# Attention with the keys on the partitions, and two output tiles of a projection begun slice by slice

## The reference, cut to what matters

```python
# first block: projection of the heads' output, y_b is 1040 x 1024
merged = (jax.nn.sigmoid(p[..., o5:o6]) * (y_a @ w_ssm_proj[l])
          + jax.nn.sigmoid(p[..., o6:]) * (y_b @ w_hgrn_proj[l]))

# second block: 8 heads, 1024 queries, 1280 keys (256 of the context), 96 dims, 64 values
def one(qi):
    s = jnp.einsum('bqhd,bkhd->bhqk', qi, k, preferred_element_type=jnp.float32) * scale
    p = jax.nn.softmax(s, axis=-1).astype(v.dtype)
    return jnp.einsum('bqhk,bkhd->bqhd', p, v)
...
yd = attn * jax.nn.silu(d_gate)
```

## Time and profile before

| | us |
|---|---|
| median of three runs (lowest, highest) | 3601.41 (3597.78, 3604.99) |
| the profiled execution | 3603.62 |
| its span in the profile | 3601.8 |
| TensorE busy | 3289.2 (91%) |
| VectorE busy | 2008.2 (56%) |
| ScalarE busy | 943.8 (26%) |
| GpSimd busy | 227.4 (6%) |
| TensorE idle in heads_out ahead of L795 | 35.6 |
| exponentials of the attention, first to last start | 3031.7 to 3391.1 |

### The profile page before, as it was taken

The page is one execution under the profiler, slowest core; times in us unless marked ns, Lnnn a source line. Parts: engine busy times, 40 slices in busy tenths (PEclk is TensorE's granted clock), DMA queues, the critical chain, the costliest instruction groups (busy, mean ns, idle before and its releaser), DMA issues. The chain is left out here.

```text
span 3601.8 us, 47693 instructions
## 1 busy us (share of the span) xinstructions
PE 3289.2 (91%) x20158; PEld 3042.2 (84%) x20158; DVE 2008.2 (56%) x2814; ACT 943.8 (26%) x1178; POOL 227.4 (6%) x224
## 2 busy tenths in 40 slices
PE   3999999999688779999999999899988996988887
PEld 3999999999677679999999999899988983555465
DVE  5565655566568444566446446645445535666446
ACT  3222222222323331121111111221133314444323
POOL 0000000000005200000000000000012000222200
PEclk9999999999798789999999999999989997999898
DMA  3222222222343344321321321411121321000031
GB/s 100 91 78 75 90 85 86 90 89 74 137 102 50 95 170 135 129 77 53 106 81 46 108 79 38 153 37 43 50 74 37 128 87 74 1 1 1 22 133 69
DMA packets 102463, 285.76 MB, mean 79 GB/s; under 512 B 13157, under 2 KB 32101, under 8 KB 101993
## 3 DMA queue, kind: packets, MB, share of 16 engines
q1 hardware_dynamic: 102248, 282.70, 24.6%
HBM read 218.68 MB, written 63.98 MB: 78 GB/s over the span
## 5 line engine op out<-in xcount | busy, mean ns | idle before, releaser
L491 PE MATMUL mixer_in_dense<-mix_z_high,mixer_in_whigh 128*128 128x348 f32 x1344 | 445.8, 332 | 11.3 <-POOL mixer_in_out L328 11.3
L491 PE MATMUL mixer_in_dense<-mix_z_high,mixer_in_wlow 128*128 128x348 f32 x1344 | 439.1, 327 | 0.0
L491 PE MATMUL mixer_in_dense<-mix_z_low,mixer_in_whigh 128*128 128x348 f32 x1344 | 438.2, 326 | 0.0
L1372 PE MATMUL flow_dense<-rst_norms_operand_b_high,flow_whigh 128*128 128x342 f32 x1248 | 399.2, 320 | 0.4 <-DVE flow_wlow L1464 0.4
L1372 PE MATMUL flow_dense<-irst_norms_operand_b_low,flow_whigh 128*128 128x342 f32 x1248 | 398.3, 319 | 0.0
L1372 PE MATMUL flow_dense<-rst_norms_operand_b_high,flow_wlow 128*128 128x342 f32 x1248 | 397.4, 318 | 0.0
L1930 PE MATMUL joint_dense<-rst_norms_operand_b_high,joint_whigh 128*128 128x342 f32 (+2 forms) x1056 | 344.7, 326 | 17.0 <-DVEq L2047 10.1
L1930 PE MATMUL joint_dense<-rst_norms_operand_b_high,joint_wlow 128*128 128x342 f32 (+2 forms) x1056 | 341.7, 324 | 0.0
L1930 PE MATMUL joint_dense<-irst_norms_operand_b_low,joint_whigh 128*128 128x342 f32 (+2 forms) x1056 | 340.6, 323 | 0.0
L1372 PE MATMUL flow_dense<-first_operand_a_high,flow_whigh 128*128 128x342 f32 (+1 forms) x912 | 291.4, 320 | 26.9 <-DVEq L1485 26.9
L1372 PE MATMUL flow_dense<-first_operand_a_low,flow_whigh 128*128 128x342 f32 (+1 forms) x912 | 291.8, 320 | 0.0
(11 more groups left out here) (544 smaller groups left out, 6201.3 us busy)
## 6 DMA issues: line engine op xcount, KB each, us to landing
mixer_in_wstage<-w_in SPq DMA_DIRECT2D x56, 512.0 KB, 4.6
mixer_in_mod_w<-w_mod SPq DMA_DIRECT2D x64, 384.0 KB, 3.6
first_norms_weights<-w_up SPq DMA_DIRECT2D x44, 512.0 KB, 3.5
flow_side<-h SPq DMA_DIRECT2D x24, 512.0 KB, 4.3
h<-flow_out SPq DMA_DIRECT2D x24, 512.0 KB, 3.2
first_norms_weights<-ab_w_in SPq DMA_DIRECT2D x20, 512.0 KB, 3.6
p<-mixer_in_out SPq DMA_DIRECT2D x16, 528.0 KB, 2.9
first_norms_weights<-w_down SPq DMA_DIRECT2D x16, 512.0 KB, 3.5
```

The lines of the kernel that those rows point to most:

```text
L491: mm = pe.matmul(pd[s % 2][:, 0:W], a[n % 2][:, P * m:P * (m + 1)], z[x][:, m, W * b:W * (b + 1)], start=m == 0 and i == 0, stop=m == DT - ...
L1372: mm = pe.matmul(o, w[n % NW][:, P * k:P * (k + 1)], x[h][:, k, where], start=k == 0 and e == 0, stop=k == kt - 1 and e == 2)
```

## The change

**heads_out.** `RING` is 6. TensorE computes slices 0 to 5 (tiles 0 and 1) together: for each piece k of `yb` 18 matmuls instead of 3, then slices 6 to 23 as before. The weights of tile 1 are loaded behind the first `yb` piece, and their high and low parts made ahead of piece 1. The small pieces of VectorE move in the table: one power behind each of the pieces 4, 5 and 6 and four behind the last, turns from 0 to 1, rotation and reverse from 1 to 2, coefficients from 2 to 3, the first table from 3 to 4, and later ones by about one slice.

**attend.** The work is in 16 units U of 512 queries of one head. `peak` computes high x high scores of 128 queries into three banks, of which VectorE takes only the maximum (`largest`); `rows` turns four such columns of maxima into a row of 512 by a product with the negated identity, and ScalarE copies it to one more row (number 96) of `query_high`, beside a row of ones in `key_high`. `chunk` k then computes the scores with 128 keys on the partitions and 512 queries on the free axis, the maximum already subtracted by the extra row; ScalarE makes exp straight into the operand of the value products, ten of 128x512 a unit. No transposes, no copies and no scaling by GpSimd are left. The sum over keys is made by four adds (`add_keys`) on GpSimd and a product with ones (`key_sums`) that spreads it over 64 partitions; VectorE's `finish` takes its reciprocal, multiplies it by the gate, adds the two halves of the value sums and multiplies.

The heads_out part, of the table `at` one line (turns 0 to 1, rotation and reverse 1 to 2, coefficients 2 to 3, table 3 to 4):

```diff
-    W, NP, NQ, RING = NM // 3, NPAIR, 8, 4
+    W, NP, NQ, RING = NM // 3, NPAIR, 8, 6
...
-                       (0, "turns", 0), (1, "rotation", 0), (1, "reverse", 0), (2, "coefficients", 0), (2, "negate", 0),
+                       (1, "turns", 0), (2, "rotation", 0), (2, "reverse", 0), (3, "coefficients", 0), (4, "table", 0),
...
                 for m in range(4):
                     load_yb(m)
+                    if m == 0:
+                        load(1)
                 for m in range(4, HH):
                     sp.wait_ge(x_low, m - 3)
                     load_yb(m)
-                load(1)
...
                 high(0)
                 for m in range(HH):
+                    if m == 1:
+                        high(1)
                     act.wait_ge(yb_landed[m % 4], 16 * (m // 4 + 1))
...
-                        if n + 1 < DT:
+                        if n and n + 1 < DT:
                             high(n + 1)
...
-                for s in range(NS):
+                def products(s, k):
                     n, b = divmod(s, 3)
-                    if b == 0:
-                        pe.wait_ge(low_ready, n + 1)
-                    if s >= RING:
-                        pe.wait_ge(moved, s - RING + 1)
+                    for e, (w, v) in enumerate(((wh, 0), (wl, 0), (wh, 1))):
+                        mm = pe.matmul(pd[s % RING][:, 0:W], w[n % 2][:, P * k:P * (k + 1)],
+                                       x[v][:, k, FIRST + W * b:FIRST + W * (b + 1)],
+                                       start=k == 0 and e == 0, stop=k == DT - 1 and e == 2)
+                    return mm
+
+                for k in range(DT):
+                    pe.wait_ge(x_low, k + 1)
+                    for s in range(6):
+                        if k == 0 and s % 3 == 0:
+                            pe.wait_ge(low_ready, s // 3 + 1)
+                        mm = products(s, k)
+                        if k == DT - 1:
+                            mm.then_inc(full, 1)
+                for s in range(6, NS):
+                    if s % 3 == 0:
+                        pe.wait_ge(low_ready, s // 3 + 1)
+                    pe.wait_ge(moved, s - RING + 1)
                     for k in range(DT):
+                        mm = products(s, k)
                     mm.then_inc(full, 1)
...
                 low(0)
                 for m in range(HH):
+                    if m == 1:
+                        low(1)
                     dve.wait_ge(x_high, m + 1)
...
-                    if b == 1 and n + 1 < DT:
+                    if n and b == 1 and n + 1 < DT:
                         low(n + 1)
```

The attention, its new functions and schedule:

```diff
+    def unit(U):
+        own = [[("e", U, k)] for k in range(NKT)]
+        first_, second_, third_ = made_at(U)
+        if U == 0:
+            for k in range(NKT):
+                own[k].append(("v", k))
+        if U + 1 < UNITS:
+            for q, k in enumerate((1, 3, 5, 7)):
+                own[k].append(("peak", U + 1, q))
+            own[6].append(("rows", U + 1, 0))
+        if U:
+            for p, k in enumerate((2, 3, 5, 7)):
+                own[k].append(("sums", U - 1, p))
+        own[2] += first_
+        own[4] += second_
+        own[8] += third_
+        if U + 1 < UNITS:
+            own[9].append(("rows", U + 1, 1))
+        if U:
+            own[9] += [("keys", U - 1), ("sums", U - 1, 4)]
+        return [n for k in own for n in k]
...
+        def add_keys(ch, tt, U):
+            p = PT[U % 2]
+            ch.do(tt(acc[:, :, :], p[:, 0:5, :], p[:, 5:10, :], ALU.add))
+            ch.do(tt(acc[:, 0:2, :], acc[:, 0:2, :], acc[:, 2:4, :], ALU.add))
+            ch.do(tt(acc[:, 0, :], acc[:, 0, :], acc[:, 1, :], ALU.add))
+            ch.do(tt(acc[:, 0, :], acc[:, 0, :], acc[:, 4, :], ALU.add))
...
+                def peak(U, q):
+
+                    h, b = divmod(U, 2)
+                    i = 4 * U + q
+                    if i:
+                        pe.wait_ge(maxed, i)
+                    q0 = HALF * b + P * q
+                    for k0, w in ((0, 512), (512, 512), (1024, 256)):
+                        mm = pe.matmul(pS[:, k0:k0 + w], qh[h % 2][0:KD, q0:q0 + P], kh[h % 2][0:KD, k0:k0 + w],
+                                       start=True, stop=True, skip_group_check=True)
+                    mm.then_inc(peaked, 1)
...
+                def rows(U, r):
+                    if U and r == 0:
+                        pe.wait_ge(rows_in, U)
+                    for q in (2 * r, 2 * r + 1):
+                        i = 4 * U + q
+                        pe.wait_ge(maxed, i + 1)
+                        mm = pe.matmul(pR[:, P * q:P * q + P], mx[:, i:i + 1], minus[:, :], start=True, stop=True,
...
+                def chunk(n):
+                    _, U, k = n
+                    h, b = divmod(U, 2)
+                    j, at, keys = h % 2, half_of(U), slice(P * k, P * k + P)
+                    if k == 0:
+                        pe.wait_ge(lows, HL.at(h, f"rope{b}"))
+                            pe.wait_ge(ones_in, 2)
+                        pe.wait_ge(rows_in, U + 1)
                     o = wait_free(pe, n)
+                    pe.matmul(o, kh[j][0:KD + 1, keys], qh[j][0:KD + 1, at], start=True, stop=False)
+                    pe.matmul(o, kl[j][0:KD, keys], qh[j][0:KD, at], start=False, stop=False)
+                    pe.matmul(o, kh[j][0:KD, keys], ql[j][0:KD, at], start=False, stop=True).then_inc(full, 1)
...
+                def value_sums(U, p):
+                    h = U // 2
+                    if p == 0:
+                        if U == 0:
+                            pe.wait_ge(v_made, 1)
+                        else:
+                            pe.wait_ge(y_added, U)
+                        pe.wait_ge(exped, NKT * (U + 1))
+                    for g in range(2):
+                        k = 2 * p + g
+                        mm = pe.matmul(pY[VD * g:VD * (g + 1), :], V[:, k, VD * h:VD * (h + 1)], PT[U % 2][:, k, :],
+                                       start=p == 0, stop=p == 4, skip_group_check=True)
+                    if p == 4:
+                        mm.then_inc(y_full, 1)
...
+                def key_sums(U):
+                    pe.wait_ge(added, U + 1)
+                    if U:
+                        pe.wait_ge(inverted, U)
+                    pe.matmul(pK, c["ones"][:, 0:VD], acc[:, 0, :], start=True, stop=True).then_inc(keys_full, 1)
...
+                def row(U):
+                    act.wait_ge(rows_full, U + 1)
+                    act.activation(qh[U // 2 % 2][KD:KD + 1, half_of(U)], pR, ACT.Copy).then_inc(rows_in, 1)
...
+                def largest(U, q):
+                    i = 4 * U + q
+                    dve.wait_ge(peaked, i + 1)
+                    dve.tensor_reduce(mx[:, i:i + 1], pS[:, 0:T2], AX.X, ALU.max).then_inc(maxed, 1)
+
+                def finish(U):
+                    h, at, own = U // 2, half_of(U), rows_of(U)
+                    dve.wait_ge(keys_full, U + 1)
+                    ch.do(dve.reciprocal(ri[own, :], pK))
+                    dve.sem_inc(inverted, 1)
+                    if U == 0:
+                        dve.wait_ge(gates_in, 64)
+                    ch.inc(tt(ri[own, :], ri[own, :], dg[own, h // 2, at], ALU.mult))
+                    dve.wait_ge(y_moved, U + 1)
+                    if h >= 2:
+                        dve.wait_ge(y_low, 2 * (h // 2 - 1) + U % 2 + 1)
+                    ch.do(tt(yp[own, at], pY[own, :], ytmp[own, :], ALU.add))
+                    dve.sem_inc(y_added, 1)
+                    ch.do(tt(yp[own, at], yp[own, at], ri[own, :], ALU.mult))
+                    dve.sem_inc(y_ready, 1)
...
+                ch = Chain(pool, pstep)
+                for U in range(UNITS - 1):
+                    pool.wait_ge(exped, NKT * (U + 1))
+                    if U:
+                        pool.wait_ge(keys_full, U)
+                    add_keys(ch, pool.tensor_tensor, U)
+                    pool.sem_inc(added, 1)
```

365 lines of the change are left out of this document (148 added, 217 removed).

## The result

The changed kernel takes 3658.18 us (median of 4 runs, 3656.11 to 3663.77) against 3599.6 us for the kernel before on the same chip: a ratio of 1.017 (95% interval 1.0156 to 1.0183), or 58.6 us more. Forecast were 3654, 53 above the median then known. The profiled execution has a span of 3654.7 us, 52.9 more than the one before.

A forecast was written before the change was run, and what follows sets the result against it. TensorE was taken to bound both changed places, its idle time being what could be won. Terms -12 (heads_out), +10 (finish) and +53 (hold) sum to +51; with 1 to 3 more at the end units, 3654 us, range 3590 to 3690.

The forecast's parts named there:

- The hold: Attention: GpSimd's adds lock the shared SBUF port against finish's product with the gate; TensorE waits 3.6 us a unit, +53.
- The reciprocal at 3.3 us: Attention, finish: VectorE's reciprocal of 64x512 takes 3.3 us, from 6.2 ns an element in the old rows.
- +10 without the hold: Attention: finish's chain alone exposes 1.2 us a unit, making units 23.2 us and the tail 2 to 3 longer.
- rival 1: No collision: GpSimd's adds meet finish too late or share the port without holding it; 3600 us, chance 0.13.
- The unit: Attention: 20.7 us of TensorE work at clock 0.94, plus 3.6 and 1.3 of waits, 26.9 or 27 a unit.
- The beginning: Attention: its beginning was taken to be about equal in length to before.
- heads_out: heads_out: slices 0 to 5 together keep TensorE busy; one wait of about 15 us for wlow, -12.
- rival 2: Attention: finish's chain is covered, a unit takes about 21.2 us; 3567 to 3580 us, chance 0.14.
- rival 3: Attention: GpSimd keeps the port through all four adds, VectorE never between; about 3690 to 3710 us, chance 0.10.
- A reading of the rows: Attention before: TensorE's 33.5 us idle ahead of transposes was put down to copies out of their banks.

The follow-up runs named there:

- the late adds: Changed kernel with GpSimd's adds of a unit waiting for the end of the previous unit's finish instead of its key sum: 3602.07 us, ratio 1.002.
- the heads_out part alone: Changed heads_out with attention as in the kernel before: 3578.27 us, ratio 0.995; run once more, 3574.98 us, ratio 0.9943.
- `finish` spread: Changed kernel with finish cut into pieces by urgency and its products of two SBUF inputs on GpSimd: 3567.48 us, ratio 0.991; once more 3564.43 us.
- the late adds and the copy: Changed kernel with GpSimd's adds waiting for the previous finish and a copy in place of the reciprocal: 3561.18 us, ratio 0.9895.
- the copy: Changed kernel with a copy in place of finish's reciprocal, leaving out the division by the sum: 3648.51 us, ratio 1.0151.
- `y_added` first: Changed kernel with finish reordered: sum of the two value halves first, then reciprocal, gate product, last product: 3657.2 us, ratio 1.0158.

## Why the prediction was right

- **The hold.** Right in mechanism and place, and shown: with the adds moved, or with one operand in another memory, L2733 falls to 0.69 and 51 to 57 us go, for a forecast of 53. Right in size at the wait, 3.5 us 14 times against 3.6, in part by two misses that cancel: `y_added` comes 6.6 us after the reciprocal's start, sooner than the 7.3 to 7.5 behind the key sum, and TensorE stands at its wait 3.3 us after that start instead of 3.8 behind the key sum.
- **The reciprocal at 3.3 us.** Right, 3.35. The Trainium skill (VectorE: DVE Perf Modes, "First, the fixed hardware budget") gives a repeat count of 8 and no duration. Read as eight passes over 512 elements, which was my reading and an estimate, it made 4.3 us; the trace does not bear that out: 3.35 us for 512 elements is 6.5 ns each.
- **+10 without the hold.** Mis-sized: with the late adds, and with the gate product reading PSUM, attention costs 24 and 26 us over the heads_out part alone. That their times, 3602.07 and 3601.04, stand at rival 1's 3600 is luck, since the kernel before took 3594.7 and 3594.5 beside them, 7 us less than the 3601.4 that the forecast started from, and heads_out gained more than 12. Written out, the +10 had only 5.6 for the units and 2 to 3 for the tail, 8 in all. What it lacked is in the late adds' trace: middle units of 24.9 us instead of 23.2 (TensorE idle 2.9 us in each instead of 1.2, at clock 0.94), and a first unit of 29.0 instead of 22.8, while the way to the first exponential is 2 to 3 shorter.
- **The unit.** Forecast 27, measured 28.6 in the middle. The mis-sized term is the clock on TensorE's own work. Its idle time is near the forecast: 4.6 us a unit, 3.5 of them for `y_added`, where 3.6 and 1.3 had been added. I took 20.7 us of work at a clock of 0.94, but the granted clock was 0.86, and 20.7/0.86 is 24.1 instead of 22.0, +2.1 a unit. The new instructions are not the reason: with each of TensorE's gaps taken off and the granted clock counted, its work in the twelve middle units comes to 20.5 to 20.8 us at full clock in all nine runs with this attention (an estimate from their traces), and the stretches at 0.50 stand behind the waits.
- **The beginning** was not equal. From TensorE's first product of the attention to the first exponential it takes 27.5 us (2976.4 to 3003.9) instead of 30.3, and the first unit behind it 29.0 instead of 22.8: 3 longer together.
- **heads_out.** -15.6 for -12. The wait for `wlow` was 13.3 for 15, and the second one, counted at up to 3, did not come.
- **The total.** It is nearer to the forecast than its parts, and that is luck. Attention costs +78 by the profiles and +81 alone, 12 to 17 over the forecast. In the profiles 4 more of heads_out and 9 of differences between executions stand against it.
- **The rivals.** The covered chain (rival 2) is not what this kernel does, but it was the right picture of what it could do: with `finish` spread a unit takes 21.8 over all and 22.2 in the middle, with the late adds and the copy 21.5 and 21.8, near the 21.2 that rival had. GpSimd did not keep the port (rival 3): in each unit VectorE got in behind the first add and behind the second.
- **A reading of the rows.** The waits ahead of the transposes were put down to the copies out of their banks. The earlier trace rows has 11.8 of the 33.5 us there; 11.2 stand with L2665, an increment behind VectorE's work on the queries, and 6.5 with GpSimd's scaling.

## What to carry to other kernels

When work goes to GpSimd, look for VectorE operations that read two SBUF tiles in the same stretch: here each waited for the rest of the GpSimd instruction that it met, up to 5.47 us for a product of 0.69 (with the copy). Price that from any place in the old trace where the two have met, and either start GpSimd's part later, give VectorE one operand in PSUM, or put such products on GpSimd too. And a shorter link in a chain is worth nothing while another holds the end of it: the reciprocal's 2.7 us were worth 0 in a unit with the hold, and 41 us over all without it. And the wait has a second price: TensorE's clock fell behind it here, so that taking the wait off gave back more than its length.

## What had not been expected of the hardware

- GpSimd's adds are longer too where VectorE's product is under way: that of 1024 elements took 2.68 us instead of 2.35, that of 512 behind it 1.60 instead of 1.27. VectorE came in between the first and the second add and between the second and the third, in every unit where they met.
- In the changed kernel the granted clock fell to 0.50 during or just behind each wait of 3.3 to 3.6 us that TensorE had for `y_added`. Together these stretches come to 92 us of 326, against 34 with the late adds, whose waits for `y_added` are 1.5 us: some 29 us of TensorE's time beside the 28 us of waiting itself. The longer wait is not always the dearer one: with `y_added` first TensorE is idle 5.9 us in each middle unit instead of 4.6, and has 75 us at 0.50.
